# A two-layer decoder step: x first, then the scale block in two halves, and six units ahead of the shift block

## The reference, cut to what matters

```python
mod = (c @ w_ada[l] + b_ada[l]).reshape(B, N_SUB, 3, D_MODEL)[:, :, :, None, :]
h = ada_norm(x, norm_gain[l, 0], mod[:, 0, 0], mod[:, 0, 1])   # rmsnorm(x, g) * (1 + scale) + shift
x = x + 0.5 * mod[:, 0, 2] * swiglu(h, w_ffn_in[l, 0], w_ffn_out[l, 0])
```

## Time and profile before

| | us |
|---|---|
| median of 3 runs | 1436.14 (1436.05 to 1436.6) |
| span of the profiled execution, first to last instruction | 1434.9 |
| median of the runs less this span | 1.24 |
| TensorE busy | 1420.2 |

### The profile page before, as it was taken

The page is one execution under the profiler, slowest core; times in us unless marked ns, Lnnn a source line. Parts: engine busy times, 40 slices in busy tenths (PEclk is TensorE's granted clock), DMA queues, the critical chain, the costliest instruction groups (busy, mean ns, idle before and its releaser), DMA issues.

```text
span 1434.9 us, 33152 instructions
## 1 busy us (share of the span) xinstructions
PE 1420.2 (99%) x13908; PEld 1359.6 (95%) x13908; DVE 950.0 (66%) x1651; ACT 812.2 (57%) x1350; POOL 98.9 (7%) x154
## 2 busy tenths in 40 slices
PE   8999999999999999999999999999999999999998
PEld 6999999998999999999999999999999999999997
DVE  5764547779876697555575545587898677955553
ACT  3554435877676476344464444468876755744543
POOL 3030000011110210000000000000011002000000
PEclk9999999999999999999999999999999999999999
DMA  9998787689994669787669898776999557785661
GB/s 340 312 275 267 246 264 205 179 241 275 232 239 133 199 187 293 220 247 249 196 202 269 271 282 258 191 205 194 260 252 266 167 155 218 222 241 159 178 187 51
DMA packets 460414, 323.75 MB, mean 226 GB/s; under 512 B 11668, under 2 KB 436069, under 8 KB 460266
## 3 DMA queue, kind: packets, MB, share of 16 engines
q1 hardware_dynamic: 452240, 299.96, 71.8%
q0 software_dynamic: 7584, 20.51, 5.4%
q10 hardware_dynamic: 442, 1.17, 0.2%
HBM read 313.29 MB, written 8.37 MB: 224 GB/s over the span
## 4 chain that ended last, share of the span: by engine, by line
PE 91%; DVE 4%; issue 2%; ACT 1%; DMA 1%; SPq 1%; DVEq 0%; ACTq 0%
PE bank L513 28%; PE bank L514 27%; PE bank L515 27%; PE bank L704 4%; DVE wlo L478 1%; PE bank L920 1%; DMA scale_tiles<-in_w_ada 1%; SPq L577 1%; PE bank L948 1%; PE bank L967 1%; DVE x L1976 0%; PE bank L989 0%; PE bank L924 0%; PE bank L743 0%; PE bank L1010 0%
## 5 line engine op out<-in xcount | busy, mean ns | idle before, releaser
L478 DVE TENSOR_TENSOR wlo<-raw,whi 128x1024 fp32r<-128x1024 f32 (+1 forms) x432 | 513.3, 1202 | 325.3 <-ACT whi L470 323.9
L513 PE MATMUL bank<-hH,whi 128*128 128x264 f32 x2016 | 577.9, 287 | 0.0
L514 PE MATMUL bank<-hL,whi 128*128 128x264 f32 x2016 | 571.5, 283 | 0.0
L515 PE MATMUL bank<-hH,wlo 128*128 128x264 f32 x2016 | 570.9, 283 | 0.0
L470 ACT ACTIVATE whi<-raw 128x1024 fp32r<-128x1024 f32 (+1 forms) x432 | 438.1, 1033 | 172.9 <-PE bank L515 168.4
L513 PEld LDWEIGHTS bank<-hH,whi 128*128 128x128 f32 x2016 | 379.6, 188 | 13.4 <-issue 12.4
L514 PEld LDWEIGHTS bank<-hL,whi 128*128 128x128 f32 x2016 | 379.9, 188 | 0.0
L515 PEld LDWEIGHTS bank<-hH,wlo 128*128 128x128 f32 x2016 | 378.1, 188 | 0.0
L513 PE MATMUL bank<-hidH,whi 128*128 128x264 f32 x704 | 200.6, 285 | 0.0
L515 PE MATMUL bank<-hidH,wlo 128*128 128x264 f32 x704 | 200.1, 284 | 0.0
L514 PE MATMUL bank<-hidL,whi 128*128 128x264 f32 x704 | 199.5, 283 | 0.0
(11 more groups left out here) (372 smaller groups left out, 1718.6 us busy)
## 6 DMA issues: line engine op xcount, KB each, us to landing
raw<-in_w_ffn_in SPq DMA_DIRECT2D x172, 512.0 KB, 4.9
raw<-in_w_in SPq DMA_DIRECT2D x120, 512.0 KB, 6.1
ring<-in_w_ada SPq DMA_DIRECT2D x96, 512.0 KB, 6.9
raw<-in_w_ffn_out SPq DMA_DIRECT2D x64, 512.0 KB, 4.9
raw<-in_w_ada SPq DMA_DIRECT2D x32, 512.0 KB, 3.7
raw<-in_w_ffn_out SPq DMA_DIRECT2D x32, 384.0 KB, 4.9
raw<-in_w_out SPq DMA_DIRECT2D x16, 512.0 KB, 5.0
out<-st POOLq DMA_DIRECT2D x12, 512.0 KB, 8.0
```

What stands on the lines that cost most here:

```text
L478: nc.vector.tensor_tensor(wlo[:, s, 0:w], raw_unit(n)[:, 0:w], whi[:, s, 0:w].bitcast(F), ALU.subtract).then_inc(lo_done, 1)
L513: nc.tensor.matmul(out, a, rh, start=start, stop=False)
L514: nc.tensor.matmul(out, a, rl, start=False, stop=False)
L515: return nc.tensor.matmul(out, b, rh, start=False, stop=stop)
```

## The change

The transfers of x go to SyncE and come first. The scale block is loaded and multiplied as two halves of 512 columns (`scale_load`, `scale_units`): each half is four transfers of 512 KB, whose rows are 2 KB long and not 4 KB. The first half gives the gains of contraction tiles 0 to 3 (`half_gains(0)`), and `first_units(k, 0)` multiplies these four tiles for units 0, 1 and 2. The second half follows, with `first_units(k, 1)`. `HF` goes from 4 to 6: units 4 and 5 also run without the shift, and their loads stand ahead of shift tiles 8 and 12. `raw_first` still holds four units (`HR`); units 4 and 5 lie in the normal raw tiles 4 and 5, which `shift_products` must have read before units 10 and 11 may be loaded, so SyncE waits for it there. The bank results of units 4 and 5 lie in `ring` tile 3 until pair 2 is done (`hid_lo`), and SyncE waits for that before it loads that tile.

```diff
-HY, HM, HF = 8, 8, 4
-FILL, KEEP = 38, 4
+HY, HM, HF, HR = 8, 8, 6, 4
+FILL, FILL_X, KEEP = 16, 12, 4
 U_IN, U_OUT, U_MIX = 2 * FT, 3 * KT, 82
 OUT_K = (8, 8, 6)
...
                 if n < FIRST:
-                    if FIRST_BEFORE[n]:
-                        sp.wait_ge(first_in[FIRST_OF[n]], FIRST_BEFORE[n])
-                    sp.dma_start(first_tile(n), src).then_inc(first_in[FIRST_OF[n]], 16)
+                    sp.wait_ge(scale_in[n % 4], 16 * (n // 4))
+                    if n >= 12:
+                        wait(sp, "ada_used", 0, 7)
+                    sp.dma_start(shift_tiles[:, n - 8], src).then_inc(scale_in[n % 4], 16)
                 else:
                     load(sp, "a", n, raw[:, raw_of("a", n)], src)
 
+            def scale_load(h, q):
+
+                if h:
+                    sp.wait_ge(scale_in[q], 16)
+                src = w_ada[0, 256 * q:256 * q + 256, D + 512 * h:D + 512 * h + 512]
+                sp.dma_start((scale_a, scale_b)[h][:, 2 * q:2 * q + 2],
+                             src.rearrange("(k p) n -> p k n", p=P)).then_inc(scale_in[q], 16)
+
             def in_load(L, f, k):
 
                 n = unit(L, f"in{f}", k)
+                if n in (HR + RAW, HR + 1 + RAW):
+                    sp.wait_ge(set_pe, 5)
                 col = k // 2 * P + (k % 2) * FFN
                 load(sp, "m", n, r3(raw_unit(n), KT),
                      w_ffn_in[L, f, :, col:col + P].rearrange("(k p) n -> p k n", p=P))
...
+                if n == FIRST + 3:
+                    wait(sp, "hid_lo", 0, HF // 2 - 1)
...
-            for n in range(6):
-                ada_load(n)
+            for t in range(2):
+                sp.dma_start(stage[:, t, :], x_prompt[0, t * P:(t + 1) * P, :]).then_inc(set_load[1], 16)
+            scale_load(0, 0)
+            scale_load(0, 1)
             in_load(0, 0, 0)
-            ada_load(6)
-            ada_load(7)
+            scale_load(0, 2)
+            scale_load(0, 3)
             in_load(0, 0, 1)
             in_load(0, 0, 2)
             sp.wait_ge(set_pe, 1)
-            for n in range(8, 11):
+            for q in range(4):
+                scale_load(1, q)
+            in_load(0, 0, 3)
+            in_load(0, 0, 4)
+            for n in range(8, 12):
                 ada_load(n)
-            in_load(0, 0, 3)
-            for n in range(11, 16):
+            in_load(0, 0, 5)
+            for n in range(12, 16):
                 ada_load(n)
-            for kind, n in LOADS[4:]:
...
-            pe.wait_ge(set_dve, 1)
-            ada_units(0, 2)
-            mm(AUX[1][0:32, 0:T], ones[:, 0:32], ones[:, :], start=True, stop=True)
+            def scale_units(h, q):
+
+                pe.wait_ge(scale_in[q], 16 * h + 16)
+                for kt in (2 * q, 2 * q + 1):
+                    src = (scale_a, scale_b)[h][:, kt, :].rearrange("p (b j i) -> p j b i", j=4, i=32)
+                    for j in range(4):
+                        last = mm(AUX[h][32 * j:32 * j + 32, 0:128].rearrange("p (b i) -> p b i", i=32),
+                                  cst[:, kt], src[:, j], start=(kt == 0), stop=(kt == KT - 1))
+                    if h:
+                        last.then_inc(S["ada_used"], 1)
+                if h == 0 and q == 3:
+                    last.then_inc(half_pe, 1)
+
...
 
                 pe.wait_ge(set_dve, SHIFT_IN)
-                for kt in range(KT):
-                    src = raw_first[:, :, kt * P:(kt + 1) * P].rearrange("p u (j i) -> p j u i", i=32)
-                    for j in range(4):
-                        last = mm(AUX[0][32 * j:32 * j + 32, 0:32 * HF].rearrange("p (u i) -> p u i", i=32),
-                                  shift_s[:, kt], src[:, j], start=(kt == 0), stop=(kt == KT - 1))
+                for tiles, col, n in ((raw_first, 0, HR), (raw[:, HR:HF], 32 * HR, HF - HR)):
+                    for kt in range(KT):
+                        src = tiles[:, :, kt * P:(kt + 1) * P].rearrange("p u (j i) -> p j u i", i=32)
+                        for j in range(4):
+                            last = mm(AUX[0][32 * j:32 * j + 32, col:col + 32 * n].rearrange("p (u i) -> p u i", i=32),
+                                      shift_s[:, kt], src[:, j], start=(kt == 0), stop=(kt == KT - 1))
                 last.then_inc(set_pe, 1)
+
+            def first_units(k, half):
+
+                n = unit(0, "in0", k)
+                unit_ready(pe, n)
+                for kt in range(4 * half, 4 * half + 4):
+                    pe.wait_ge(set_dve, u0_lo(kt))
+                    last = mm3(BK[k][:, 0:NT], n % SLOTS, kt * P, uH[:, kt, 0:NT], uL[:, kt, 0:NT], kt == 0, kt == KT - 1)
+                if half:
+                    last.then_inc(unit_done, 1)
 
             def ffn(L, f):
                 si, so = f"in{f}", f"out{f}"
...
@@ -817,14 +870,11 @@
                             wait(pe, "h_lo", L, f * 8 + kt // 2)
                         last = mm3(BK[b][:, 0:NT], n % SLOTS, kt * P, hH[:, kt], hL[:, kt], kt == 0, kt == KT - 1)
                     last.then_inc(unit_done, 1)
-                    if (L, f, k) == (0, 0, 0):
-                        ada_units(8, 2)
-                        spread_root(0, 0)
-                    if (L, f, k) == (0, 0, 1):
-                        ada_units(10, 2)
-                    if (L, f, k) == (0, 0, 2):
+                    if (L, f, k) == (0, 0, 3):
+                        ada_units(8, 4)
+                    if (L, f, k) == (0, 0, 4):
                         ada_units(12, 4)
-                    if (L, f, k) == (0, 0, 3):
+                    if (L, f, k) == (0, 0, 5):
                         shift_products()
                     if (L, f, k) == (0, 0, 10):
                         parameter_rows()
...
+            first_units(0, 0)
+            scale_units(1, 0)
+            first_units(1, 0)
+            scale_units(1, 1)
+            scale_units(1, 2)
+            first_units(2, 0)
+            scale_units(1, 3)
+            spread_root(0, 0)
+            for k in range(3):
+                first_units(k, 1)
             for L in range(NL):
                 ffn(L, 0)
                 mixer(L)
...
```

More of the change, by code:

```diff
@@ L366, in trunk @@
         ring_in = sem("ring_in")
-        first_in = [sem(f"first_in{i}") for i in range(len(FIRST_GROUPS))]
+        scale_in = [sem(f"scale_in{i}") for i in range(4)]
+        half_pe, half_dve = sem("half_pe"), sem("half_dve")
         hi_done = sem("hi_done")
@@ L682, in _ @@
             last.then_inc(set_pe, 1)
+            for i in range(FILL_X):
+                mm(AUX[i % 2][0:32, 0:32], ones[:, 0:32], ones[:, 0:32], start=True, stop=True)
             def ada_units(n0, count):
@@ L691, in ada_units @@
                         pe.wait_ge(set_dve, BIAS_T)
+                    if n == 8:
+                        wait(pe, "ada_turned", 0, 0)
                     if n < FIRST:
-                        pe.wait_ge(first_in[FIRST_OF[n]], FIRST_COUNT[n])
-                        tile = first_tile(n)
+                        pe.wait_ge(scale_in[n % 4], 16 * (n // 4 + 1))
+                        tile = shift_tiles[:, n - 8]
                     elif b in RING_OF:
@@ L785, in ffn @@
                     wait(pe, "ada_turned", 0, ADA_BLOCKS.index((L, 7)))
-                for k in range(U_IN):
+                for k in range(3 if (L, f) == (0, 0) else 0, U_IN):
                     n = unit(L, si, k)
@@ L2431, in mixer, with half_gains @@
                 u_low(L, 1, KT - 1)
-            split_lo(dve, 0)
-            to_mod(0)
-            wait(dve, "mod_ready", 0, 0)
-            gains(0, 0)
-            wait(dve, "G_ready", 0, 0)
-            tt(us[:, :], x[:, :, T:NT], Gs[:, :, 1:9], ALU.mult).then_inc(set_dve, 1)
-            dve.wait_ge(set_act, X_COPIED)
-            for k in range(KT):
-                dve.wait_ge(set_act, U0_HI + k + (k > 0))
-                v.scalar_tensor_tensor(uL[:, k, 0:T], x[:, k, 0:T], Gs[:, k, 0:1], uH[:, k, 0:T].bitcast(F),
-                                       ALU.mult, ALU.subtract).then_inc(set_dve, 1)
-                if k == 0:
-                    dve.wait_ge(set_dve, U0_S)
-                    dve.wait_ge(set_act, U0_HI + 1)
-                    tt(uL[:, :, T:NT], us[:, :], uH[:, :, T:NT].bitcast(F), ALU.subtract).then_inc(set_dve, 1)
+            def half_gains(half):
+                k = slice(4 * half, 4 * half + 4)
+                if half:
+                    wait(dve, "ada_used", 0, 7)
+                    v.transpose(adaT[:, 128:256], AUX[1][:, 0:128]).then_inc(S["ada_turned"], 1)
+                    wait(dve, "ada_turned", 0, 0)
+                else:
+                    dve.wait_ge(half_pe, 1)
+                    v.transpose(adaT[:, 0:128], AUX[0][:, 0:128]).then_inc(half_dve, 1)
+                    dve.wait_ge(half_dve, 1)
+                done = (half_dve, S["mod_ready"])[half]
+                c0_ = PC["bada"] + 8 + 4 * half
+                tt(mod[:, 8 + 4 * half:12 + 4 * half],
```

(47 more changed lines are left out.)

80 lines of the change are left out of this document (44 added, 36 removed).

## The result

| | before | after |
|---|---|---|
| median of 4 runs each, us | 1436.22 (1436.05 to 1436.6) | 1448.74 (1447.68 to 1449.06) |
| span of the profiled execution, us | 1434.9 | 1446.9 |
| TensorE busy, us | 1420.2 | 1423.6 |

The ratio of after to before is 1.0084, 95% interval 1.0072 to 1.0096: slower by 0.84% or 12.5 us, where 2.2 were forecast. TensorE's idle time grew from 14.7 to 23.3 us, its busy time by 3.4.

What follows compares the result with a forecast made beforehand. TensorE, busy 1420.2 of 1434.9 us, and a full DMA early on were taken as the bounds. A ring group 2.2 us later gave span 1437.1, plus 1.24 to the median: 1438.3 us, range 1435.3 to 1440.4.

Steps and rivals of the forecast that it cites:

- Step (1): At the front: half a block suffices to start; first unit product near 17 us against 23.31, gain about 2.9 us.
- Step (2): Up to the shift block: TensorE hardly waits for the last shift tile and ends unit 5 near 44.1 us.
- Step (3): Before `shift_products`: unit 6's splits delay the copy to `shift_s`; start at 46.8 us, a new wait of 2.7 us.
- Step (4): In `shift_products`: 64 more records add 1.2 us to 1.96; it ends at 49.9 us, the change 1.2 us behind.
- the sum: At the ring group: 83.3 - 81.1 = +2.2 us on the span, with nothing differing afterwards; 1438.3 us.
- Step (5): Unit 10's load waits until 49.9 us, lands near 54.0; last ring tile near 83.3, TensorE waits 1.0 us more.
- Step (6): Costed at nothing: third early pair's extra operations, wait before ring tile 3, fewer unread products, x on SyncE.
- D: Rival: the clock falls in the wait before `shift_products`, slowing it and the ring; +3.8 us, 1439.9; chance 0.09.

Runs made afterwards that it cites:

- e4: e1 with the product of the second half's last tile pair placed ahead of unit 2's first half on TensorE; 1438.5 us, ratio 1.0011 to before.
- e3: e1 with ring tiles 0 to 2 issued ahead of unit 10's load; 1437.62 us, ratio 1.0007 to before.
- e1: After with FILL 26 for 16: ten more unread products (40 instructions) at the start; 1439.89 us, ratio 1.0023 to before.
- e2: Before with FILL 28 for 38: ten fewer unread products (40 instructions) at the start; 1446.48 us, ratio 1.0069 to before.
- e11: After with FILL 21 for 16: five more unread products (20 instructions) at the start; 1444.09 us, ratio 1.0052 to before.
- e12: After with FILL 6 for 16: ten fewer unread products (40 instructions) at the start; 1444.18 us, ratio 1.0051 to before.
- e7: e2 with GpSimd's state transfers cut to 16 of 128 partitions, except layer 0's first two loads; 1444.46 us, ratio 1.0052 to before.
- e9: After with the units of w_in loaded as 16 of 128 partitions, same TensorE instructions; 1443.39 us, ratio 1.0048 to before.
- e10: e9 with GpSimd's state transfers also cut to 16 of 128 partitions, except the first two loads; 1440.44 us, ratio 1.0025 to before.

## Why the prediction was wrong, step by step

- Step (1): the front gains 2.9 us. The first product with a unit came at 19.78, not 17, and the second halves began at 29.68, not 26.7, both 3 us late. I had put the chain directly behind the landings; TensorE had more in its list. The last tiles of half a were multiplied at 16.49, behind the first squares of x, which waited for ScalarE. A quarter of the second half stood behind unit 2's first half (e4 turned that round, and the second halves began at 27.96), and VectorE's turning behind that. So the front gained next to nothing; the work that went ahead is what I said, but it started later than I said.
- Step (2): TensorE's times are all late by step (1)'s 3 us (`shift_products` reached at 47.3, not 44.1). The landing it sets beside them is right: unit 6 at 42.5 for 42.7.
- Step (3): "46.8", the copy to `shift_s`, measured 46.62. "A wait of 2.7 us": there is none in after, since step (1)'s 3 us made TensorE come at 47.3 by itself. The gate is real (1.23 us in e4), but that `shift_products` started near 46.8 is luck: the late front put TensorE there at about the time at which the gate would have opened.
- Step (4): "1.2" for the extra products. The second group's row has 1.08 for its 64 records, but its start lies 1.77 behind the first's, so both together took 2.85 us where the sum had 3.16. That made up for most of the 0.54 us by which they started later: done at 50.19 for 49.9.
- Step (5): right in its mechanism and size. Issue 50.25 (49.9), landing 54.0 (54.0), last ring tile 83.8 (83.3), wait 1.31 (1.0), offset 2.85 (2.2). e3 confirms the cause. The same wait was 1.3 to 2.3 us in the six kernels with this front, so that it came out within 0.3 us in after is partly chance.
- Step (6), costed at nothing: no wait for the split of unit 11 or for ring tile 3 stands among TensorE's waits; right. One item of it, however, was the fault: "Fewer unread products at the start lie before x has landed" priced their time and not their number.
- **The step that failed** is the last sentence of the sum: "From there on nothing distinguishes the two kernels". Two things did: how many instructions TensorE had behind it when it reached the mixers, and with that where its blocks end. The missing term is 3.4 + 3.1 us of waits and some 1.7 us of low clock behind each, 9.9 us, against 12.0 - 2.2 = 9.8 seen. With the sum's +2.2 it gives +12.1. e1 takes this term out of after, and e2 puts it into before. None of the rivals had it, and the range ended at 1440.4. D priced a fall of the clock, but before `shift_products`, where it did not happen.

What is left of the result without this term is what was forecast: e1, after without the gaps, takes 2.9 us more than before (1439.89 against 1437.01) where the sum had 2.2; that agreement rests in part on the errors of steps (1) and (3), which cancel.

What stays open. Which point of the program asks for a block, and how far ahead, no view shows directly; the 36 records above are inferred. The runs show that the waits go when the borders move 40 instructions the right way or when the transfers around them thin out; how their length depends on the border's place in between (e11, e12) isn't explained. That the two sorts of transfers can replace each other as the cause rests on e7, e9 and e10, at one phase for each kernel. Whether the block waits in the queues of the DMA engines or for memory wasn't tried.

## What to carry to other kernels

When an edit changes the number of TensorE's instructions, even by products that nobody reads, look for waits put down to "issue" (no releaser) in dense stretches of small products under a full DMA, however far they are from the edit; try two or three paddings of a few dozen instructions before an order is judged, or one phase's luck is taken for the order's worth. A load made to wait for a late consumer leaves a bubble in a full DMA, which is paid at the next place where TensorE has no slack: have other loads issued ahead of the wait. And price what stands in an engine's list between a landing and the work that it releases.

## What the runs showed of the hardware

- TensorE's instructions arrive in packets of 16 KB, one for 256 of its records (the places of the waits are multiples of 256 apart), and the profile counts them among the time of the same 16 DMA engines as the data. Under a share of 1.1 such a packet started 0.9 us after TensorE had run dry (after), and in all ten waits TensorE went on 2.4 to 2.7 us after the packet's start.
- A wait of 3.40 or 3.10 us was followed by 3.4 us at 1.2 GHz, and after one of 2.29 us (e10) a mean granted clock of 0.83 showed; after waits of 1.31 and 2.05 us (after, e1) it stayed at 1.00 at the same place. The length of the wait alone does not decide: after 2.27 us in e12's second mixer it fell to 0.50 for 3.4 us, after 2.63 us in e7's it stayed at 1.00.
- Fewer bytes elsewhere make the remaining transfers take their place: with the states cut, the weights' share from 355 to 366 us rose from 66.3% (e2) to 71.9% (e7).
